# The final norm of an encoder layer, taken by halves of a row, with the reciprocal root applied on ScalarE and VectorE

## The chip, the cores and the metric

The kernel runs on one core of one Trainium2 chip. Its metric is the device time of one execution in microseconds (us). A core has TensorE (PE, with its weight loads as PEld), VectorE (DVE), ScalarE (ACT), GpSimd (POOL) and SyncE (SP), each with an instruction stream of its own that runs in order; they wait for one another through semaphores. Work arrays lie in SBUF, in 128 partitions; products of TensorE arrive in PSUM, here 8 banks of 128x512 f32.

## What is computed

One layer of a bidirectional encoder on 768 tokens (a group of 512 and one of 256) of width 1024: a token mixer, a feed-forward block, and a last RMSNorm. Cut to what matters here:

```
def rmsnorm(x, w):
    xf = x.astype(F32)
    y = xf * lax.rsqrt(jnp.mean(xf * xf, axis=-1, keepdims=True) + EPS)
    return (y * w.astype(F32)).astype(x.dtype)

    for l in range(DEPTH):                      # DEPTH is 1
        h = h + token_mixer(rmsnorm(h, norm_mix[l]), ...)
        h = h + conv_ffn(rmsnorm(h, norm_ffn[l]), ...)
    return rmsnorm(h, norm_final)
```

The mean of the squares runs over a whole row of 1024, so no element of a row can leave before the row's last residual is added. The weight `norm_final` does not depend on the mean.

## The kernel before, in words

The tokens are six tiles of 128 (`NT` = 6), the width is 8 pieces of 128. `h[:, t, :]` is the residual row of tile `t`, 128x1024 f32, in SBUF from the middle of the program on. Each matrix product is made of three passes of float32r halves (hi, lo), so a weight comes from HBM into `raw`, is split by ScalarE (`split_hi`, `hi_unit`) and VectorE (`split_lo`, `lo_unit`) into `ring`, and TensorE reads it there.

The feed-forward block works in three chunks of `FF`, with 8, 8 and 6 blocks of 128. After each chunk, `down` multiplies the gated activations `g` by the down weights and VectorE adds the result to `h` (`residual`, L1122). It does so in two halves of the output columns: first columns 0 to 511 for all six tiles, then columns 512 to 1023. In the last chunk the second half runs tile by tile (`by_token`): TensorE makes 18 matmuls of 128x512 for tile 0 and counts `down_done` up, then 18 for tile 1, and so on. The order in every stream is written out by hand; no scheduler moves anything.

Behind the last chunk stands the final norm. `wfin`, the weights of it in all partitions, is loaded over `af` as soon as the last product that reads `af` is done. Then, tile by tile, in this order:

- VectorE adds the second half of the row (L1122);
- ScalarE squares the row of 1024 into `junk2` and sums it into `stat[:, 0, t]` (L786);
- VectorE divides by 1024 and adds EPS (`variance`, L800), ScalarE takes the root (L788), VectorE the reciprocal (L1317);
- VectorE multiplies the row of 1024 by the reciprocal and by `wfin`, in place in `h` (L1319), and counts `out_ready` up;
- SP, which waits for that, issues the store of the tile to `y_s` or `y_p` (L396). The program ends when all six stores have landed.

Of the kernel before, what the change touches and what calls it, by code (L numbers as in the profile page):

```python
# [30 lines left out]
ALU = mybir.AluOpType  # L31
ACT = mybir.ActivationFunctionType
F32 = mybir.dt.float32
# [3 lines left out]
P = 128  # L37
D = 1024
KD = D // P
NS, NP = 512, 256  # L40
T = NS + NP
NT = T // P
# [6 lines left out]
EPS = 1e-6  # L49
STRIP = NS + 3 * P  # L50
UNIT = 1024
HALF = T // 2
HK = KD // 2
PIECE = UNIT // 2
CHUNKS = ((0, 8), (8, 16), (16, 22))
# [29 lines left out]
ORD, PLACE, UPLACE, FREED, PIECES = {}, {}, {}, {}, {}  # L85
# [79 lines left out]
def build(nc, x_s, x_p, units, pairs, vec, w_final, ident_d, masks_d, rot_d, strips_d, y_s, y_p):  # L165
    with ExitStack() as ctx:
        def sem(name):
            return ctx.enter_context(nc.semaphore(name))

        def persistent(name, shape, dtype=F32):  # L170
            return ctx.enter_context(nc.sbuf_tensor(name, shape, dtype))

        def region(*tensors):

            with ExitStack() as phase:
                return [phase.enter_context(nc.sbuf_tensor(n, s, d)) for n, s, d in tensors]
# [2 lines left out]
        ring = persistent("ring", [P, 8, 2, PIECE], F32R)  # L179
        ident = persistent("ident", [P, P])  # L180
        vecs = persistent("vecs", [P, V_N])
        stat = persistent("stat", [P, 4, NT])

        hn, x_in, xn, y32, junk = region(
            ("hn", [P, 2, KD, T], F32R),
# [13 lines left out]
        _, osq, _, kT = region(  # L199
            ("d0", [P, 2 * KD * T + KD * T + 2048 + 2 * T + 7 * P + T], F32), ("osq", [P, 2, T], F32),  # L200
            ("d1", [P, 10 * T], F32), ("kT", [P, T], F32))
# [5 lines left out]
        _, merged = region(("n2", [P, 2 * KD * T], F32), ("merged", [P, 2, KD, T], F32R))  # L207


        h, hxn, hy = region(("h", [P, NT, D], F32), ("hxn", [P, 2, D], F32), ("hy", [P, 6, KD, P], F32))  # L210
        _, g, raw2, tb, u2, v2, cb, mid, af = region(
            ("b0", [P, NT, D], F32), ("g", [P, 2, 8, T], F32R), ("raw2", [P, 2, UNIT], F32), ("tb", [P, 2, PIECE], F32),
            ("u2", [P, 2, T], F32), ("v2", [P, T], F32), ("cb", [P, T], F32), ("mid", [P, HALF], F32),
            ("af", [P, 7, 2, HK, HALF], F32R))
        *_, wfin, junk2 = region(
            ("c0", [P, NT * D + 2 * 8 * T + 3072 + 4 * T + HALF], F32), ("wfin", [P, D], F32), ("junk2", [P, D], F32))

        _, sums0 = region(
            ("e0", [P, NT * D + 2 * 8 * T + 3072 + 4 * T + HALF], F32), ("sums0", [P, 7, 2, HK, HALF], F32))
# [6 lines left out]
        vec_ld, mix_ld, strip_ld, fin_ld, out_st = sem("vec_loaded"), sem("mix_loaded"), sem("strip_loaded"), sem("fin_loaded"), sem("out_stored")  # L226
# [3 lines left out]
        sq_done, var_done, sd_done, xn_done, tr_done, y_done, yhi_done, ylo_done = (  # L230
            sem(n) for n in ("sq_done", "var_done", "sd_done", "xn_done", "tr_done", "y_done", "yhi_done", "ylo_done"))
# [11 lines left out]
        w_done, h_up = sem("wout_done"), sem("h_updated")  # L243
# [5 lines left out]
        s_done, s_last, fyhi, fylo = sem("tokens_combined"), sem("last_tokens_combined"), sem("forms_hi"), sem("forms_lo")  # L249
        p1_cp, p12_cp, p13_cp = sem("first_copied"), sem("second_copied"), sem("third_copied")  # L250
        c11_dn, c22_dn, c12_dn = sem("c11_done"), sem("c22_done"), sem("c12_done")
        dn, out_rdy = sem("down_done"), sem("out_ready")

        raws = (raw, raw2)

# [66 lines left out]
        @blk.sync  # L322
        def _(sp):
            def load(n, parity):

                after(sp, lo_split, n - 1)
                src = units[n] if isinstance(n, int) else units[at(n), :, :].rearrange("a p n -> (a p) n")
                sp.dma_start(raw[:, parity, :], src).then_inc(raw_ld[parity], 16)

            xs = x_s.rearrange("(t p) d -> t p d", p=P)  # L330
            xp = x_p.rearrange("(t p) d -> t p d", p=P)
            for t in range(NT):
                sp.dma_start(x_in[:, t, :], xs[t] if t < 4 else xp[t - 4]).then_inc(x_ld[t], 16)

            def mixer_loads(hd):
                for u in range(U_MIX):
                    load(hd * U_MIX + u, u % 2)
                    if u == 5:

                        after(sp, rp, 12 * hd)  # L340
                        src = strips_d[hd] if isinstance(hd, int) else strips_d[at(hd), :, :].rearrange("a p n -> (a p) n")
                        sp.dma_start(strips[:].rearrange("p a n -> p (a n)"), src).then_inc(strip_ld, 16)

            mixer_loads(0)
            with sp.Fori(1, HEADS_H) as hd:
                mixer_loads(hd)
            with sp.Fori(U_HG // 2, (U_O0 + 4) // 2) as i:
                load(2 * i, 0)
                load(2 * i + 1, 1)

            sp.wait_ge(unit_done, U_O0)
            sp.dma_start(h[:, 0:4, :], x_s.rearrange("(t p) d -> p t d", p=P)).then_inc(h_ld, 16)
            sp.dma_start(h[:, 4:6, :], x_p.rearrange("(t p) d -> p t d", p=P)).then_inc(h_ld, 16)

            with sp.Fori((U_O0 + 4) // 2, U_D // 2) as i:
                load(2 * i, 0)
                load(2 * i + 1, 1)

            def load_pair(i, prior, plain):

                b = raw_of(i)
                if prior is not None:
                    sp.wait_ge(flo, ORD[prior, A22] + 1)
                else:
                    sp.wait_ge(lo_split, plain + 1)
                sp.dma_start(raws[b][:, 0, :], pairs[i, 0]).then_inc(pu_ld[b], 16)
                if prior is not None:
                    sp.wait_ge(flo, ORD[prior, S4] + 1)
                sp.dma_start(raws[b][:, 1, :], pairs[i, 1]).then_inc(pv_ld[b], 16)

            for lo, hi in CHUNKS:
                for i in range(lo, hi):
                    if i == 1:

                        sp.wait_ge(w_done, 2 * NT)
                        sp.dma_start(raw2[:, 0, :], pairs[i, 0]).then_inc(pu_ld[1], 16)
                        sp.dma_start(raw2[:, 1, :], pairs[i, 1]).then_inc(pv_ld[1], 16)
                    elif i == 0 or i == lo + 1:
                        load_pair(i, None, U_D + lo - 1)
                    else:  # L380
                        load_pair(i, i - 2, None)
                last_raw = hi - 1 if raw_of(hi - 1) == 0 else hi - 2
                for n in range(U_D + lo, U_D + hi):
                    if n < U_D + lo + 2:
                        sp.wait_ge(flo, ORD[last_raw, S4] + 1)
                    else:
                        sp.wait_ge(lo_split, n - 1)
                    sp.dma_start(raw[:, n % 2, :], units[n]).then_inc(raw_ld[n % 2], 16)

            sp.wait_ge(fdone, len(ORD))  # L390
            sp.dma_start(wfin[:], w_final).then_inc(fin_ld, 16)
            ys = y_s.rearrange("(t p) d -> t p d", p=P)
            yp = y_p.rearrange("(t p) d -> t p d", p=P)
            for t in range(NT):
                sp.wait_ge(out_rdy, t + 1)
                sp.dma_start(ys[t] if t < 4 else yp[t - 4], h[:, t, :]).then_inc(out_st, 16)  # L396
            sp.wait_ge(out_st, 16 * NT)


# [1 line left out]
        def _(act):  # L401
# [353 lines left out]
            for lo, hi in CHUNKS:  # L755
# [25 lines left out]
                for n in range(U_D + lo, U_D + hi):  # L781
                    hi_upto(UPLACE[n] + 6)
            for t in range(NT):
                act.wait_ge(h_up, (2 + 2 * len(CHUNKS)) * NT - NT + t + 1)
                act.drain()
                act.activation(junk2[:], h[:, t, :], ACT.Square, accum_out=stat[:, 0, t:t + 1]).then_inc(sq_done, 1)  # L786
                act.wait_ge(var_done, 2 * NT + t + 1)
                act.activation(stat[:, 2, t:t + 1], stat[:, 1, t:t + 1], ACT.Sqrt).then_inc(sd_done, 1)  # L788


        @blk.vector
        def _(dve):
# [5 lines left out]
            def variance(t, base):  # L798
                dve.wait_ge(sq_done, base + t + 1)
                dve.tensor_scalar(stat[:, 1, t:t + 1], stat[:, 0, t:t + 1], 1.0 / D, EPS, ALU.mult,  # L800
                                  ALU.add).then_inc(var_done, 1)
# [472 lines left out]
            for c, (lo, hi) in enumerate(CHUNKS):  # L1274
# [32 lines left out]
                if c + 1 < len(CHUNKS):  # L1307
                    for t in range(NT):
                        dve.wait_ge(dn, 2 * NT * c + NT + t + 1)
                        residual(t, 1, t)  # L1310
            dve.wait_ge(fin_ld, 16)
            for t in range(NT):
                dve.wait_ge(dn, (2 * len(CHUNKS) - 1) * NT + t + 1)
                residual(t, 1, t)
                variance(t, 2 * NT)
                dve.wait_ge(sd_done, 2 * NT + t + 1)
                dve.reciprocal(stat[:, 3, t:t + 1], stat[:, 2, t:t + 1])  # L1317
                dve.drain()
                dve.scalar_tensor_tensor(out=h[:, t, :], in0=h[:, t, :], scalar=stat[:, 3, t:t + 1], in1=wfin[:],  # L1319
                                         op0=ALU.mult, op1=ALU.mult).then_inc(out_rdy, 1)  # L1320


        @blk.gpsimd
# [501 lines left out]
```

## Time and profile before

| | us |
|---|---|
| median of 3 runs | 1285.16 |
| the runs | 1284.92 to 1285.38 |
| the profiled execution, its own time | 1284.88 |
| its span, first to last instruction | 1283.1 |
| mean granted TensorE clock | 0.996 |

The profiled execution took 1.8 us more than its span, which lies outside the instructions, and 0.28 us less than the median. TensorE is busy for nearly the whole span; busy times of the others overlap it. The profile page divides the span into 40 slices of 32 us, so the whole final norm lies in the last slice, and it has to be read from the timeline. In a row of the timeline or of the chain the first number is the start and the second the length, both in us from the span's start; in brackets stands how long the engine had been idle, and what ended that.

### The profile page before, as it was taken

Reading aid. Unit: us, or ns where it says so; the run is one execution under the profiler, and the core shown is the slowest. Engines: PE = TensorE matmul, PEld = TensorE weight load, DVE = VectorE, ACT = ScalarE, POOL = GpSimd, SP = SyncE. Lnnn points to the kernel's source line nnn. Section 1 sums busy time; section 2 is a strip of 40 time slices with the busy share of each in tenths; the row PEclk is TensorE's granted clock in tenths of the full one; section 3 lists DMA queues with packets and bytes.
Section 4 is the critical chain, followed back from the end, with each engine's and each line's share of the span. In section 5 each row is a group of like instructions: output and inputs, shape, how many; then the busy total and the mean of one; then the engine's idle time right before and its main releaser. Section 6 shows DMA issues by size and latency. Waiting matters only on the chain.

```text
span 1283.1 us, 17974 instructions
## 1 busy us (share of the span) xinstructions
PE 1251.8 (98%) x7088; PEld 1127.2 (88%) x7088; DVE 708.1 (55%) x956; ACT 484.4 (38%) x706; POOL 129.0 (10%) x93
## 2 busy tenths in 40 slices
PE   6999999999999999999999989999999999999997
PEld 5999999899999988888888879998789998799976
DVE  7494585486377372232223697765237764347654
ACT  5352253335144152122211355553125553135522
POOL 0000000000000000000000304420133420223200
PEclk9999999999999999999999998999999999999999
DMA  4311211101211112212124122122202213112122
GB/s 168 134 42 42 74 38 50 61 33 49 78 33 49 34 50 66 66 50 68 63 67 164 33 66 66 66 66 82 82 34 66 77 55 125 40 37 79 50 82 98
DMA packets 23179, 86.09 MB, mean 67 GB/s; under 512 B 2512, under 2 KB 2768, under 8 KB 23120
## 3 DMA queue, kind: packets, MB, share of 16 engines
q1 hardware_dynamic: 22544, 83.90, 19.0%
q10 hardware_dynamic: 576, 1.38, 0.3%
q8 instruction: 41, 0.67, 0.2%
q14 instruction: 18, 0.15, 0.0%
HBM read 82.12 MB, written 3.15 MB: 66 GB/s over the span
## 4 chain that ended last, share of the span: by engine, by line
PE 94%; DVE 4%; ACT 1%; DVEq 1%; issue 1%; DMA 0%; SPq 0%; ACTq 0%
PE ps L1397 58%; PE ps L1641 24%; PE ps L1494 3%; PE ps L1434 3%; PE ps L1487 1%; PE ps L1504 1%; PE ps L1422 1%; DVE af L1182 1%; PE ps L1424 1%; DVE h L1122 1%; DVE ring L1135 1%; PE ps L1379 0%; PE ps L1470 0%; PE ps L1475 0%; PE ps L1479 0%
## 5 line engine op out<-in xcount | busy, mean ns | idle before, releaser
L1397 PE MATMUL ps<-hn,ring 128*128 128x256 f32 (+1 forms) x2544 | 466.8, 338 | 0.3 <-DVE hn L824 0.3
L1397 PEld LDWEIGHTS ps<-hn,ring 128*128 128x128 f32 x2544 | 387.2, 189 | 51.6 <-issue 0.7
L1641 PE MATMUL ps<-af,ring 128*128 128x384 f32 x1848 | 332.6, 341 | 10.8 <-DVE v L1219 5.6
L1641 PEld LDWEIGHTS ps<-af,ring 128*128 128x128 f32 x1848 | 328.3, 189 | 14.9 <-issue 5.9
L1397 PE MATMUL ps<-ring,g 128*128 128x512 f32 x792 | 186.7, 397 | 0.8 <-issue 0.8
L1397 PEld LDWEIGHTS ps<-ring,g 128*128 128x128 f32 x792 | 148.9, 188 | 37.8 <-issue 2.0
L795 DVE TENSOR_TENSOR ring<-raw,ring 128x1024 fp32r<-128x1024 f32 x68 | 83.1, 1224 | 122.1 <-ACT ring L409 117.7
L458 ACT ACTIVATE sig<-ps 128x768 f32<-128x768 f32 x36 | 29.2, 810 | 183.1 <-PE ps L1397 183.0
L409 ACT ACTIVATE ring<-raw 128x1024 fp32r<-128x1024 f32 x68 | 71.6, 1055 | 29.8 <-PE ps L1397 10.6
L1135 DVE TENSOR_TENSOR ring<-raw,ring 128x512 fp32r<-128x512 f32 x88 | 73.4, 869 | 16.7 <-ACT ring L646 16.6
L1356 POOL TENSOR_TENSOR sums<-raw 128x512 f32<-128x512 f32 x1 | 1.3, 1295 | 713.8 <-DMA raw<-in_pairs 713.8
L1397 PE MATMUL ps<-gated,ring 128*128 128x512 f32 (+1 forms) x384 | 69.1, 338 | 0.0
L1397 PE MATMUL ps<-ring,merged 128*128 128x512 f32 x288 | 68.8, 398 | 0.1
L1397 PEld LDWEIGHTS ps<-gated,ring 128*128 128x128 f32 x384 | 59.6, 188 | 8.8
L1397 PEld LDWEIGHTS ps<-ring,merged 128*128 128x128 f32 x288 | 53.8, 188 | 13.2 <-issue 0.5
L873 DVE TENSOR_TENSOR pt<-ps,strips 128x512 f32<-128x512 f32 (+1 forms) x48 | 28.5, 601 | 66.1 <-PE ps L1424 66.1
L646 ACT ACTIVATE ring<-raw 128x512 fp32r<-128x512 f32 x88 | 52.3, 622 | 30.2 <-PE ps L1397 30.2
L1122 DVE TENSOR_TENSOR h<-ps,h 128x512 f32<-128x512 f32 x48 | 33.1, 690 | 42.7 <-PE ps L1397 42.2
L471 ACT ACTIVATE yc<-tree_k 128x768 f32<-128x768 f32 x28 | 25.6, 916 | 76.6 <-DVE tree_k L960 41.2
L1135 DVE TENSOR_TENSOR ring<-tb,ring 128x512 fp32r<-128x512 f32 x63 | 43.4, 693 | 17.8 <-ACT ring L646 17.8
L1227 DVE SCALAR_TENSOR_TENSOR cb<-u,vecs,cb 128x511 f32<-128x511 f32 x88 | 50.2, 612 | 2.0 <-issue 0.4
L1140 DVE TENSOR_TENSOR ring<-raw,ring 128x1024 fp32r<-128x1024 f32 x22 | 27.6, 1264 | 40.9 <-ACT ring L653 40.9
(151 smaller groups left out, 1210.1 us busy)
## 6 DMA issues: line engine op xcount, KB each, us to landing
raw<-in_units SPq DMA_DIRECT2D x90, 512.0 KB, 3.5
raw<-in_pairs SPq DMA_DIRECT2D x44, 512.0 KB, 3.4
strips<-in_strips SPq DMA_DIRECT2D x4, 896.0 KB, 4.5
x_in<-in_x_s SPq DMA_DIRECT2D x4, 512.0 KB, 5.4
h<-in_x_s SPq DMA_DIRECT2D x1, 2048.0 KB, 8.3
y_s<-h SPq DMA_DIRECT2D x4, 512.0 KB, 2.6
x_in<-in_x_p SPq DMA_DIRECT2D x2, 512.0 KB, 7.5
h<-in_x_p SPq DMA_DIRECT2D x1, 1024.0 KB, 10.4
```

The costliest lines, as they stand in the source:

```text
L409: act.activation(ring[:, 2 * slot:2 * slot + 2, 0, :], pieces(raw[:, slot % 2, :]), ACT.Copy).then_inc(hi_split, 1)
L458: ins = act.activation(sig[:, u % 2, :], dense(u), ACT.Sigmoid)
L646: act.activation(place_of(i, x, 0), source(i, x), ACT.Copy).then_inc(fhi, 1)
L795: dve.tensor_tensor(ring[:, 2 * slot:2 * slot + 2, 1, :], pieces(raw[:, slot % 2, :]), ring[:, 2 * slot:2 * slot + 2, 0, :].bitcast(F32), ...
L873: dve.tensor_tensor(pt[:, (i % 4) * NS:(i % 4) * NS + width], ps[:, 4 + i % 2, 0:width], strips[:, a, c0:c0 + width], ALU.mult).then_inc(r ...
L1122: return dve.tensor_tensor(hs, ps[:, bank, :], hs, ALU.add).then_inc(h_up, 1)
L1135: dve.tensor_tensor(place_of(i, x, 1), source(i, x), place_of(i, x, 0).bitcast(F32), ALU.subtract).then_inc(flo, 1)
L1227: ins = dve.scalar_tensor_tensor(out=cs, in0=u2[:, i % 2, c0 + frm:c0 + frm + w - 1], scalar=vecs[:, V_CONV + tap * NF + i:V_CONV + tap * ...
L1397: ins = pe.matmul(out, w if stationary_w else x, x if stationary_w else w, start=start and i == 0, stop=stop and i == 2)
L1434: ins = pe.matmul(ps[:, 6 + m // 4, col:col + 64], pt[:, (i % 4) * NS + c * P:(i % 4) * NS + (c + 1) * P], rv[:, m * P + 64 * a:m * P + 64 ...
L1494: ins = pe.matmul(out(c * P, P), yc[:, c * P:(c + 1) * P], facing(tree_q[:], what, c * P, P), start=True, stop=True)
L1641: ins = pe.matmul(ps[:, bank, 0:HALF], ring[:, p, a, k * P:(k + 1) * P], af[:, x, b, k, :], start=first and k == 0 and j == 0, stop=k == H ...
```

## The change

`stat` gets two more rows (4 and 5), `junk2` is halved, and a new tile `hw` (six rows of 1024) takes the weighted row; it lies over `af`, as `wfin` does. Four semaphores are new, and `out_first_half_ready`.

Ahead of the last six residuals, when the first halves of all rows are final, ScalarE squares the six first halves (into `stat[:, 4]`), VectorE multiplies the six first halves by `wfin` into `hw`, and then makes of the six sums a scaled sum plus EPS in one 128x6 instruction (`stat[:, 5]`). Per tile there is then: the residual, a multiplication of the second half by `wfin` into `hw` on VectorE, the square of the second half on ScalarE beside it, the variance (with `stat[:, 5, t]` where EPS stood), root and reciprocal as before. The reciprocal is applied by both engines: ScalarE scales the first half of `hw`, VectorE the second, each in place, and SP waits for both.

```
-        stat = persistent("stat", [P, 4, NT])
+        stat = persistent("stat", [P, 6, NT])
...
-            ("c0", [P, NT * D + 2 * 8 * T + 3072 + 4 * T + HALF], F32), ("wfin", [P, D], F32), ("junk2", [P, D], F32))
+            ("c0", [P, NT * D + 2 * 8 * T + 3072 + 4 * T + HALF], F32), ("wfin", [P, D], F32), ("junk2", [P, PIECE], F32), ("hw", [P, NT, D], F32))
...
             for t in range(NT):
+                sp.wait_ge(out_rdy0, t + 1)
                 sp.wait_ge(out_rdy, t + 1)
-                sp.dma_start(ys[t] if t < 4 else yp[t - 4], h[:, t, :]).then_inc(out_st, 16)
+                sp.dma_start(ys[t] if t < 4 else yp[t - 4], hw[:, t, :]).then_inc(out_st, 16)
...
             for t in range(NT):
+                act.wait_ge(h_up, (1 + 2 * len(CHUNKS)) * NT - NT + t + 1)
+                act.wait_ge(fdone, len(ORD))
+                act.drain()
+                act.activation(junk2[:], h[:, t, 0:PIECE], ACT.Square, accum_out=stat[:, 4, t:t + 1]).then_inc(half_sq, 1)
+            for t in range(NT):
                 act.wait_ge(h_up, (2 + 2 * len(CHUNKS)) * NT - NT + t + 1)
                 act.drain()
-                act.activation(junk2[:], h[:, t, :], ACT.Square, accum_out=stat[:, 0, t:t + 1]).then_inc(sq_done, 1)
+                act.activation(junk2[:], h[:, t, PIECE:D], ACT.Square, accum_out=stat[:, 0, t:t + 1]).then_inc(sq_done, 1)
                 act.wait_ge(var_done, 2 * NT + t + 1)
                 act.activation(stat[:, 2, t:t + 1], stat[:, 1, t:t + 1], ACT.Sqrt).then_inc(sd_done, 1)
+                act.wait_ge(root_done, t + 1)
+                act.wait_ge(weighed, t + 1)
+                act.activation(hw[:, t, 0:PIECE], hw[:, t, 0:PIECE], ACT.Copy, scale=stat[:, 3, t:t + 1]).then_inc(out_rdy0, 1)
...
             dve.wait_ge(fin_ld, 16)
+            dve.wait_ge(fdone, len(ORD))
+            dve.drain()
+            for t in range(NT):
+                dve.tensor_tensor(hw[:, t, 0:PIECE], h[:, t, 0:PIECE], wfin[:, 0:PIECE], ALU.mult).then_inc(weighed, 1)
+            dve.wait_ge(half_sq, NT)
+            dve.tensor_scalar(stat[:, 5, :], stat[:, 4, :], 1.0 / D, EPS, ALU.mult, ALU.add).then_inc(half_var, 1)
             for t in range(NT):
                 dve.wait_ge(dn, (2 * len(CHUNKS) - 1) * NT + t + 1)
                 residual(t, 1, t)
-                variance(t, 2 * NT)
+                dve.drain()
+                dve.tensor_tensor(hw[:, t, PIECE:D], h[:, t, PIECE:D], wfin[:, PIECE:D], ALU.mult).then_inc(weighed, 1)
+                dve.wait_ge(sq_done, 2 * NT + t + 1)
+                dve.wait_ge(half_var, 1)
+                dve.tensor_scalar(stat[:, 1, t:t + 1], stat[:, 0, t:t + 1], 1.0 / D, stat[:, 5, t:t + 1], ALU.mult,
+                                  ALU.add).then_inc(var_done, 1)
                 dve.wait_ge(sd_done, 2 * NT + t + 1)
-                dve.reciprocal(stat[:, 3, t:t + 1], stat[:, 2, t:t + 1])
-                dve.drain()
-                dve.scalar_tensor_tensor(out=h[:, t, :], in0=h[:, t, :], scalar=stat[:, 3, t:t + 1], in1=wfin[:],
-                                         op0=ALU.mult, op1=ALU.mult).then_inc(out_rdy, 1)
+                dve.reciprocal(stat[:, 3, t:t + 1], stat[:, 2, t:t + 1]).then_inc(root_done, 1)
+                dve.wait_ge(root_done, t + 1)
+                dve.tensor_scalar(hw[:, t, PIECE:D], hw[:, t, PIECE:D], stat[:, 3, t:t + 1], None, ALU.mult).then_inc(out_rdy, 1)
```

On VectorE, from the six residuals of the first halves to the store of tile 0, the stream read so before (`h_updated` counts residuals, `down_done` the tiles that TensorE has finished):

```order
L1122 TENSOR_TENSOR h<-ps,h 128x512 [waits down_done] x6
L1122 TENSOR_TENSOR h<-ps,h 128x512 [waits down_done,fin_loaded]
L800 TENSOR_SCALAR stat<-stat 128x1 [waits sq_done]
L1317 RECIPROCAL stat<-stat 128x1 [waits sd_done]
L1319 SCALAR_TENSOR_TENSOR h<-h,stat,wfin 128x1024
```

In the changed kernel the same stretch of VectorE reads:

```order
L1132 TENSOR_TENSOR h<-ps,h 128x512 [waits down_done] x6
L1325 TENSOR_TENSOR hw<-h,wfin 128x512 [waits product_done,fin_loaded]
L1325 TENSOR_TENSOR hw<-h,wfin 128x512 x5
L1327 TENSOR_SCALAR stat<-stat 128x6 [waits half_squares]
L1132 TENSOR_TENSOR h<-ps,h 128x512 [waits down_done]
L1332 TENSOR_TENSOR hw<-h,wfin 128x512
L1335 TENSOR_SCALAR stat<-stat 128x1 [waits half_variance,sq_done]
L1338 RECIPROCAL stat<-stat 128x1 [waits sd_done]
L1340 TENSOR_SCALAR hw<-hw,stat 128x512 [waits root_inverted]
```

Seven instructions stand newly between the last first-half residual and the first second-half one, and a tile has five instructions on VectorE where it had four.

On ScalarE a tile of the final norm read so before (the table load stands there once, in tile 0):

```order
L786 ACTIVATE junk,stat<-h 128x1024 [waits h_updated]
L788 ACT_TABLE_LOAD
L788 ACTIVATE stat<-stat 128x1 [waits var_done]
```

And now, with the six early squares ahead of it:

```order
L789 ACTIVATE junk,stat<-h 128x512 [waits product_done,h_updated] x6
L793 ACTIVATE junk,stat<-h 128x512 [waits h_updated]
L795 ACT_TABLE_LOAD
L795 ACTIVATE stat<-stat 128x1 [waits var_done]
L798 ACTIVATE hw<-hw,stat 128x512 [waits out_weighed,root_inverted]
```

A tile's square is half as long, and a scaling copy stands behind its root. TensorE's, GpSimd's and SP's streams have the same instructions in the same order, but for the source and the second wait of the stores. All tiles that are placed behind `stat` in SBUF (every one but `raw`, `ring`, `ident`, `vecs` and `stat`) start 64 bytes later in each partition.

## Rows read from the trace of the kernel before

**Rows 1.** The page, busy time of each engine and its share of the span.

```profile
PE 1251.8 (98%) x7088; PEld 1127.2 (88%) x7088; DVE 708.1 (55%) x956; ACT 484.4 (38%) x706; POOL 129.0 (10%) x93
```

**Rows 2.** The chain that ended last, from 1230 us: start, length, what.

```profile
1250.58 25.54 PE ps L1397 x108
...
1276.14 0.70 DVE h L1122
...
1276.92 1.16 ACT junk L786 x2
...
1278.10 0.16 DVE stat L800
...
1278.29 0.21 ACT stat L788
...
1278.52 0.16 DVE stat L1317
1278.68 0.03 DVEq L1318
```

**Rows 3.** The timeline from 1276 us: the last tile's last steps and stores.

```profile
1275.86 4.54 SPq L396 DMA_DIRECT2D y_p<-h  x2
...
1276.92 1.06 ACT L786 ACTIVATE junk<-h 128x1024 f32<-128x1024 f32 x1 [2.64 <-DVE h L1122]
1277.88 0.19 ACT L786 ACTIVATION_READ_ACCUMULATOR junk<-h 128x1 f32 x1
...
1278.76 1.28 DVE L1319 SCALAR_TENSOR_TENSOR h<-h,stat,wfin 128x1024 f32<-128x1024 f32 x1
```

**Rows 4.** DMA issues of the stretch 1276.1 to 1283.1: count, KB each, us to landing.

```profile
y_p<-h SPq DMA_DIRECT2D x2, 512.0 KB, 2.6
```

**Rows 5.** The issues of the last two stores: durations ns, first and last start.

```profile
L396 SPq DMA_DIRECT2D y_p<-h x2: 332/332/332, 1275.9 to 1280.1; - x2
```

**Rows 6.** Groups of instructions, shapes apart: count, busy us, mean ns of one.

```profile
L409 ACT ACTIVATE ring<-raw 128x1024 fp32r<-128x1024 f32 x68 | 71.6, 1055 | 29.8 <-PE ps L1397 10.6 <-PEq L1605 7.4 <-DMA raw<-in_units 6.7
L646 ACT ACTIVATE ring<-tb 128x512 fp32r<-128x512 f32 x63 | 37.0, 620 | 33.4 <-PEq L1735 14.6 <-PE ps L1397 14.6 <-DVE tb L1157 3.7
L720 ACT ACTIVATE cb<-u,vecs 128x384 f32<-128x384 f32 x22 | 15.5, 705 | 0.0
L496 ACT ACTIVATE rv<-ps 128x768 f32<-128x768 f32 x4 | 3.2, 812 | 10.9 <-PE ps L1479 10.9
L504 ACT ACTIVATE oT<-ps,vecs 128x768 f32 x3 | 2.7, 902 | 5.8 <-PE ps L1475 5.8
L307 DVE TENSOR_TENSOR hy<-hy 128x512 f32<-128x512 f32 x2 | 1.4, 693 | 0.2
L810 DVE TENSOR_SCALAR xn<-x_in,stat 128x1024 f32<-128x1024 f32 x6 | 4.5, 754 | 0.5
L816 DVE TENSOR_TENSOR y<-ps,vecs 128x1024 f32<-128x1024 f32 x6 | 7.3, 1220 | 1.3 <-PE ps L1379 1.3
L901 DVE TENSOR_SCALAR hstat<-hstat 128x6 f32<-128x6 f32 x4 | 0.7, 172 | 0.3
```

**Rows 7.** The timeline from 1225 us: residuals, first tile's norm, tile 4's residual.

```profile
1246.85 4.20 DVE L1122 TENSOR_TENSOR h<-ps,h 128x512 f32<-128x512 f32 x6 [2.52 <-PE ps L1397]
...
1255.13 0.69 DVE L1122 TENSOR_TENSOR h<-ps,h 128x512 f32<-128x512 f32 x1 [4.08 <-PE ps L1397]
1255.90 1.06 ACT L786 ACTIVATE junk<-h 128x1024 f32<-128x1024 f32 x1 [12.83 <-DVE h L1122]
...
1257.07 1.28 ACT L788 ACT_TABLE_LOAD   x1
...
1271.93 0.69 DVE L1122 TENSOR_TENSOR h<-ps,h 128x512 f32<-128x512 f32 x1 [0.32 <-PE ps L1397]
```

**Rows 8.** Busy time by stretch: PE, PEld, DVE, ACT, POOL, clock, DMA share, GB/s.

```profile
1250.50:1255.10 4.60, 4.52 (x20) 3.69 (x21) 0.55 (x1) 0.00 (x0) 0.00 (x0) 1.00 0.00 0
1255.10:1276.10 21.00, 21.00 (x90) 16.57 (x88) 11.23 (x20) 8.06 (x16) 0.00 (x0) 1.00 0.25 100
```

**Rows 9.** The load of the final weights: its issue in the timeline.

```profile
1234.39 0.43 SPq L391 DMA_DIRECT2D wfin<-in_w_final  x1
```

**Rows 10.** The load of the final weights: time to landing, by the tile's view.

```profile
DMA to landing us min/median/max: 6.5/6.5/6.5
```

More of the change, by code:

```diff
@@ L214, in build @@
             ("af", [P, 7, 2, HK, HALF], F32R))
-        *_, wfin, junk2 = region(
-            ("c0", [P, NT * D + 2 * 8 * T + 3072 + 4 * T + HALF], F32), ("wfin", [P, D], F32), ("junk2", [P, D], F32))
+        *_, wfin, junk2, hw = region(
+            ("c0", [P, NT * D + 2 * 8 * T + 3072 + 4 * T + HALF], F32), ("wfin", [P, D], F32), ("junk2", [P, PIECE], F32), ("hw", [P, NT, D], F32))
         _, sums0 = region(
@@ L251, in build @@
         c11_dn, c22_dn, c12_dn = sem("c11_done"), sem("c22_done"), sem("c12_done")
-        dn, out_rdy = sem("down_done"), sem("out_ready")
+        dn, out_rdy, out_rdy0 = sem("down_done"), sem("out_ready"), sem("out_first_half_ready")
+        half_sq, half_var, root_done, weighed = sem("half_squares"), sem("half_variance"), sem("root_inverted"), sem("out_weighed")
         raws = (raw, raw2)
```

## The prediction, made before the changed kernel ran

> **What bounds the kernel now.** I read the page first: TensorE is busy for 98% of the span, VectorE for 55%, ScalarE for 38% [rows 1]. An edit on VectorE and ScalarE can therefore pay only where TensorE is not running. TensorE's stream and its waits are untouched. The chain that ended last shows where it stops: a run of 108 matmuls ends at 1276.12 us, and behind it stand, one after the other, the last tile's residual, square, variance, root, reciprocal and the final multiplication [rows 2, 3]. The final multiplication ends at 1280.04 us (1278.76 + 1.28), the last store is issued at 1280.07 (the two issues end at 1280.40, each takes 0.33), and it lands 2.6 us later [rows 3 to 5]. So the span of 1283.1 us splits into 1276.1 in which TensorE sets the pace, 3.9 us of a serial chain for one tile, and 3.0 us of store and end. The change can shorten only those 3.9 us, unless it moves TensorE's end. That caps the whole effect near 0.3% of the time, and the true effect is below that, since half of the chain's links stay.
>
> **The path of the last tile, step by step.** I count from the residual's start at 1276.14 us [rows 2], because VectorE is idle there before and will be after.
>
> 1. Residual: 0.69 us, unchanged. ScalarE starts its square at 1276.92.
> 2. Square: now 512 elements instead of 1024. Before, the variance started 1.18 us behind the square's start (1276.92 to 1278.10) [rows 2]. The square took 1.06 us there, the same as ScalarE's plain copy of 1024 elements (1055 ns), and a copy of 512 takes 620 ns [rows 6, 3]. So half a row saves 0.435 us, and the accumulator read (0.19) stays. The variance can start at 1277.67.
> 3. Multiplication of the second half by the weights, new on VectorE, ahead of the variance. It waits for the residual and a drain; the same drain took 0.08 us behind the reciprocal (1278.68 to 1278.76) [rows 2, 3]. So it starts at 1276.91 and, at 0.69 us as for two SBUF operands of 128x512 [rows 6], ends at 1277.60. It lies under the square with 0.07 us to spare. That is the thinnest cover in the sum: if this step starts or runs 0.1 us later, only some hundredths appear on the path.
> 4. Variance, root, reciprocal: 0.58 us from 1278.10 to 1278.68 [rows 2], the same three instructions; the variance reads its addend from SBUF instead of an immediate, for which I take nothing and allow 0.05. The reciprocal ends at 1278.25.
> 5. Applying the reciprocal. Before: 1.28 us on VectorE for 1024 elements with two multiplications. Now there are two legs side by side. ScalarE: a copy of 512 with a scale read per partition. No row shows that form. The low end is the unscaled copy, 620 ns. The high end comes from the scaled and biased one of 384 elements, 705 ns, plus 128 elements at 0.85 ns (the slope from 620 to 1055 ns): 813 ns. Between them, the copy of 768 with such a scale takes 902 ns against 812 without, 0.09 us more [rows 6]. This is the same operation, so I take 0.62 + 0.09 = 0.71. With 0.04 us from VectorE's end to ScalarE's start (as between variance and root, 1278.25 to 1278.29), ScalarE ends at 1279.00. VectorE: a wait of 0.08 and a 128x512 multiplication by a scalar. Low end: half of the 754 ns that 1024 elements take; high end: 0.69, as two tensors; I take 0.754 less half of the 0.53 that two tensors of 1024 cost over 512 (1220 less 693 ns), since the 754 ns show about two elements in the time of one: 0.49 us [rows 6]. VectorE ends at 1278.82, before ScalarE, which sets the end.
> 6. SP waits for two semaphores; the later one is ScalarE's, and the other has been counted by then. I take no more than the 0.03 us that it took before. The store is issued at about 1279.04.
>
> The store now leaves 1.03 us earlier (1280.07 to 1279.04). For small handshakes that the rows don't show I take off 0.03, so **the gain is 1.0 us**. Bounds of the sum: ScalarE's leg at 0.62 gives 1.1; at 0.81, with 0.1 for a late weight multiplication and variance and 0.1 for extra waits, it gives 0.7.
>
> On step 5 the row shows a price for the scale, 90 ns in 812 [rows 6]. The Trainium skill, page "ScalarE: Activation LUTs", section "Step-by-step: what each stage is for", calls scale and bias a "free affine" that is applied ahead of the lookup, in each instruction; by that the leg would take 0.62 us and the time would be 1284.1. The trace speaks against it here, so the sum keeps the 0.09.
>
> **What lies ahead of the last tile, and its cover.** The six early squares start behind the first residuals (1246.85 on), where ScalarE is idle for 12.8 us [rows 7]. Each takes about 0.62 + 0.19 and a gap, 0.87 us, so all are done by about 1252.9. The six multiplications follow the six residuals that end at 1251.05, six times 0.69 and gaps, to about 1255.3; the weights landed at 1240.9 [rows 7, 9, 10]. The 128x6 instruction (0.17 us, as another of that shape [rows 6]) brings it to 1255.6. Before, the residual of tile 0 started at 1255.13 [rows 7], so tile 0 is now late by 0.4 to 0.5 us: the cover of 4.08 us of idle VectorE is used up and a little more. What absorbs the lag is TensorE's rhythm: 108 matmuls in 25.54 us are six tiles of 4.25 us, and the new chain of a tile holds VectorE for 2.7 us (1276.14 to 1278.82), where the old one held it for 3.9. Even with the table load of 1.28 us in tile 0 [rows 7], VectorE is free near 1259.4, when tile 1 arrives. From there on it waits for TensorE on every tile, as before only in the last two (0.32 and 0.31 us idle) [rows 7]. Nothing of the lag is left at 1276.14. TensorE doesn't wait for any of this: its tiles write banks whose last readers are the first-half residuals, done by 1251.05. I also price contention at nothing, because TensorE held its pace with VectorE busy for 11.2 and ScalarE for 8.1 of 21 us, at a granted clock of 1.00 in both stretches [rows 8].
>
> **The sum.** The profiled execution would be 1284.88 - 1.0 = 1283.9 us, its span 1282.1. It stood 0.28 below the median, so the median goes from 1285.16 to **1284.2 us**, 0.08% less.
>
> **Rivals.**
> - *The instruction count tells.* A tile has one more instruction on each engine and three more waits. If fixed parts of them come onto the path, 0.15 us each on two engines (a 693 ns operation of 512 elements against 1220 of 1024 leaves about 0.16 us that doesn't scale [rows 6]), the gain is 0.7 and the time 1284.5. For it speaks the 0.07 us of cover in step 3; against it, that path and kernel have the same number of links, and the additions lie beside them. The Trainium skill's page "VectorE: DVE Perf Modes", section "The TRN2 errata — SBUF-src ops pay a fixed extra latency per instruction", speaks against halves in this way: many small operations pay the fixed part each time. The rows agree with a fixed part; they don't put it on this path.
> - *It doesn't do what it says.* The two legs don't overlap but run one after the other (ScalarE's scaling behind VectorE's), say because a wait falls on the wrong one. Then step 5 takes 0.08 + 0.49 + 0.04 + 0.71 = 1.32 against 1.36, and only the square's 0.43 remains: 1284.7. The order of waits speaks against it, since both legs wait for the reciprocal alone.
> - *Slower: the moved tiles.* Everything behind `stat` starts 64 bytes later, also `hn`, `g` and `af`, which TensorE reads in nearly all of its 7088 matmuls. Should such a read cost more at the new start, it is on the path all the time. The point from which it decides is 1.0 us / 7088 = 0.14 ns for each matmul; at 0.5 ns the time would be 1285.16 - 1.0 + 3.5 = 1287.7. It can as well go the other way. Nothing in the trace varies with a start address, so I give it little.
> - *A new end on VectorE.* If its scalar multiplication ran like a two-tensor one and its waits cost 0.2 more, its leg ends at 1279.2 instead of ScalarE's 1279.0: 1284.4, inside the forecast's bounds.
>
> **How the numbers follow.** The forecast with the last rival, 1284.0 to 1284.5: 74%. The instruction count: 10%, 1284.5 to 1284.8. Legs in series or another lost overlap: 5%, up to 1285.2. Moved tiles: 8%, of which half beyond 0.2% slower and 1 in 100 faster by more than that. 3% for what I haven't seen. The runs before lie within 0.23 us of their median, which is as wide as the forecast's own bounds; with that and a small effect of the moved tiles either way, the range is 1283.4 to 1285.3. A measurement of this kernel can tell about 0.2% (2.6 us) from no change. The mechanism can't reach that: chances 0.02 faster, 0.94 same, 0.04 slower.
>
> **What would show it.** In the changed profile: TensorE's last matmul within 0.3 us of 1276.1 from the start; then square about 0.62 us, variance 1.53 us behind the residual's start (1.96 before), the reciprocal's end 2.11 behind it (2.54 before), ScalarE's scaled copy last at 2.86, the store at 2.9 (3.93 before). Tile 0's residual 0.4 to 0.5 us later than before, and VectorE idle ahead of each later one. The forecast is wrong if the variance waits for the weight multiplication instead of the square, if the scaled copy takes over 0.9 us, or if TensorE's end moves by more than the 1.0 us in question.

## The result, and the profile after

| | before | changed kernel |
|---|---|---|
| median, us | 1284.79 (6 runs) | 1277.76 (6 runs) |
| the runs, us | 1283.63 to 1285.38 | 1275.41 to 1278.74 |
| profiled execution, us | 1284.88 | 1277.07 |
| its span, us | 1283.1 | 1275.3 |

The ratio of the times is 0.9943, with a 95% interval of 0.9933 to 0.9954. The forecast was 1284.2 in a range of 1283.4 to 1285.3; the kernel is 7.0 us faster, not 1.0.

The page of the changed kernel, busy time of each engine, answers to [rows 1]:

```profile
PE 1244.8 (98%) x7088; PEld 1120.5 (88%) x7088; DVE 711.9 (56%) x969; ACT 490.8 (38%) x724; POOL 129.1 (10%) x93
```

VectorE and ScalarE have become busier by 4 and 6 us, as they should with more instructions. TensorE has the same 7088 matmuls and is busy for 7 us less. The timeline of the changed kernel from 1269 us (start, length, what, idle time before it) shows the last tile, to be laid beside [rows 2, 3]:

```profile
1269.31 0.69 DVE L1132 TENSOR_TENSOR h<-ps,h 128x512 f32<-128x512 f32 x1 [1.28 <-PE ps L1417]
1270.08 0.63 ACT L793 ACTIVATE junk<-h 128x512 f32<-128x512 f32 x1 [1.82 <-DVE h L1132]
1270.09 0.69 DVE L1332 TENSOR_TENSOR hw<-h,wfin 128x512 f32<-128x512 f32 x1
1270.62 0.19 ACT L793 ACTIVATION_READ_ACCUMULATOR junk<-h 128x1 f32 x1
1270.84 0.21 DVE L1335 TENSOR_SCALAR stat<-stat 128x1 f32<-128x1 f32 x1
1271.09 0.20 ACT L795 ACTIVATE stat<-stat 128x1 f32<-128x1 f32 x1 [0.28 <-DVE stat L1335]
1271.32 0.16 DVE L1338 RECIPROCAL stat<-stat 128x1 f32<-128x1 f32 x1 [0.27 <-ACT stat L795]
1271.52 0.72 ACT L798 ACTIVATE hw<-hw,stat 128x512 f32<-128x512 f32 x1 [0.23 <-DVE stat L1338]
1271.52 0.49 DVE L1340 TENSOR_SCALAR hw<-hw,stat 128x512 f32<-128x512 f32 x1
1272.27 0.33 SPq L398 DMA_DIRECT2D y_p<-hw  x1
```

From the residual's start to the store's issue it is 2.96 us, where it was 3.93. That is the 0.97 us that the change was to bring. But the residual itself starts at 1269.31 instead of 1276.14: 6.8 us of the gain lie before the norm, in TensorE's stream, which the diff doesn't touch. The chain that ended last tells where. First before (start, length, what; L1641 is the product that streams `af` through weights from `ring`, L1397 here the down product, which streams `ring` through weights from `g`):

```profile
772.71 100.44 PE ps L1641 x552
...
946.44 114.98 PE ps L1641 x648
...
1066.49 33.73 PE ps L1397 x144
...
1134.75 85.20 PE ps L1641 x480
```

and of the changed kernel (L1661 and L1417 are the same two lines):

```profile
770.77 98.10 PE ps L1661 x552
...
941.83 114.86 PE ps L1661 x648
...
1061.68 33.60 PE ps L1417 x144
...
1129.65 83.72 PE ps L1661 x480
```

The same 480 matmuls in a row, with nothing between them, take 83.72 us instead of 85.20: 174.4 ns each instead of 177.5. The difference is spread over the program. By the starts in the two chains, TensorE gains 1.94 us up to the row of 552, 2.41 in the `af` products of the first chunk from there on, 0.20 in the second chunk's, 1.57 in the third's, and 0.26, 0.29 and 0.16 in the three down products; the sum is 6.83. No wait of any size has gone; the matmuls themselves follow one another faster: 1817 neighbouring `af` matmuls are 177.4 ns apart before and 1821 are 175.3 ns apart after. The granted clock isn't it: 0.996 before and 0.997 after.

### The profile page after: what moved, and what is told of

Read it like the earlier page. It is cut to its first block, busy times and chain, and to the rows that moved or that the text cites. A ratio compares the mean times of both kernels' runs of the same rounds, so it can differ in the third digit from the quotient of the medians.

```text
span 1275.3 us, 18036 instructions
## 1 busy us (share of the span) xinstructions
PE 1244.8 (98%) x7088; PEld 1120.5 (88%) x7088; DVE 711.9 (56%) x969; ACT 490.8 (38%) x724; POOL 129.1 (10%) x93
## 4 chain that ended last, share of the span: by engine, by line
PE 94%; DVE 4%; ACT 1%; DVEq 1%; issue 1%; DMA 0%; SPq 0%; ACTq 0%
PE ps L1417 58%; PE ps L1661 24%; PE ps L1514 3%; PE ps L1454 3%; PE ps L1507 1%; PE ps L1524 1%; PE ps L1442 1%; DVE af L1192 1%; PE ps L1444 1%; DVE h L1132 1%; DVE ring L1145 1%; PE ps L1399 0%; PE ps L1490 0%; PE ps L1499 0%; PE ps L1495 0%
## 5 line engine op out<-in xcount | busy, mean ns | idle before, releaser
L1417 PE MATMUL ps<-hn,ring 128*128 128x256 f32 (+1 forms) x2544 | 465.2, 338 | 0.3 <-DVE hn L834 0.3
L1417 PEld LDWEIGHTS ps<-hn,ring 128*128 128x128 f32 x2544 | 385.7, 189 | 51.6 <-issue 0.7
L1661 PE MATMUL ps<-af,ring 128*128 128x384 f32 x1848 | 328.2, 340 | 11.1 <-DVE v L1229 5.6
L1661 PEld LDWEIGHTS ps<-af,ring 128*128 128x128 f32 x1848 | 324.0, 189 | 15.1 <-issue 5.9
L1417 PE MATMUL ps<-ring,g 128*128 128x512 f32 x792 | 186.0, 395 | 0.8 <-issue 0.8
L1417 PEld LDWEIGHTS ps<-ring,g 128*128 128x128 f32 x792 | 148.4, 188 | 37.6 <-issue 2.0
L805 DVE TENSOR_TENSOR ring<-raw,ring 128x1024 fp32r<-128x1024 f32 x68 | 83.2, 1224 | 121.4 <-ACT ring L411 117.0
L1417 PE MATMUL ps<-gated,ring 128*128 128x512 f32 (+1 forms) x384 | 68.8, 338 | 0.0
L1417 PE MATMUL ps<-ring,merged 128*128 128x512 f32 x288 | 68.6, 397 | 0.1
L1417 PEld LDWEIGHTS ps<-gated,ring 128*128 128x128 f32 x384 | 59.3, 188 | 8.8
L1417 PEld LDWEIGHTS ps<-ring,merged 128*128 128x128 f32 x288 | 53.6, 188 | 13.1 <-issue 0.5
```

Source lines behind the costliest of these rows:

```text
L805: dve.tensor_tensor(ring[:, 2 * slot:2 * slot + 2, 1, :], pieces(raw[:, slot % 2, :]), ring[:, 2 * slot:2 * slot + 2, 0, :].bitcast(F32), ...
L1417: ins = pe.matmul(out, w if stationary_w else x, x if stationary_w else w, start=start and i == 0, stop=stop and i == 2)
L1661: ins = pe.matmul(ps[:, bank, 0:HALF], ring[:, p, a, k * P:(k + 1) * P], af[:, x, b, k, :], start=first and k == 0 and j == 0, stop=k == H ...
```

## Experiments

In what follows "pace" is the mean time from one matmul's start to the next one's in the trace, over all neighbours of one kind less than 300 ns apart. It is worked out from the starts and doesn't depend on modelled ends.

**Is it the norm's code or the tiles' place?** One of the rivals was that every tile behind `stat` starts 64 bytes later. Two kernels split the change into its two parts. The first is the kernel before with the shift alone:

```
-        stat = persistent("stat", [P, 4, NT])
+        stat = persistent("stat", [P, 6, NT])
```

> The kernel before with nothing changed but stat at six rows (two unused), so that every tile behind it starts 64 bytes later, as in the changed kernel. Theory A (the start address of the tiles that TensorE reads sets its pace): this alone gives the larger part, 1278.5 to 1279.5 us, its last matmul near 1269.5 and the tail still 7.0 us long. Theory B (the new instructions of the norm or their places in the program did it): 1284.8, no gain. Theory C (the executions vary by themselves): anything between, and the runs of one kernel would spread over both.

The second is the changed kernel with its two new rows of sums in a small tile, `early`, behind `hw`, and `stat` as it was:

```
-        stat = persistent("stat", [P, 6, NT])
+        stat = persistent("stat", [P, 4, NT])
...
-        *_, wfin, junk2, hw = region(
+        *_, wfin, junk2, hw, early = region(
...
-            dve.tensor_scalar(stat[:, 5, :], stat[:, 4, :], 1.0 / D, EPS, ALU.mult, ALU.add).then_inc(half_var, 1)
+            dve.tensor_scalar(early[:, 1, :], early[:, 0, :], 1.0 / D, EPS, ALU.mult, ALU.add).then_inc(half_var, 1)
```

> The changed kernel with its two new rows of sums in a small tile of their own behind hw, so that stat keeps four rows and every tile starts where it did before. Theory A: only the shorter tail is left, 1283.8 us (1.0 below the kernel before), with TensorE's last matmul at 1276.1 from the start. Theory B: the whole gain, 1277.8.

Measured: the shift alone 1278.61 us (ratio 0.9948, 0.9931 to 0.9964). The norm alone 1284.21 us against 1284.86 of the kernel before (0.9995, 0.9985 to 1.0004), so its gain can't be told from nothing by the times. The trace of it tells: TensorE's end has not come forward (the last residual starts at 1276.54, 0.4 us later than in the kernel before), and the store is issued 2.96 us behind it.

```profile
1276.54 0.69 DVE L1132 TENSOR_TENSOR h<-ps,h 128x512 f32<-128x512 f32 x1 [1.29 <-PE ps L1417]
...
1278.75 0.72 ACT L798 ACTIVATE hw<-hw,stat 128x512 f32<-128x512 f32 x1 [0.23 <-DVE stat L1338]
1278.75 0.49 DVE L1340 TENSOR_SCALAR hw<-hw,stat 128x512 f32<-128x512 f32 x1
1279.50 0.33 SPq L398 DMA_DIRECT2D y_p<-hw  x1
```

Theory A holds: the place of the tiles gave 6.2 of the 7 us. Theory B, by which the norm's new instructions gave the whole gain, falls: they shorten the tail by about what they were priced at and leave TensorE's pace as it was. The runs of each kernel keep to themselves, 1277.04 to 1279.17 us and 1283.40 to 1284.71, which speaks against theory C.

**Other shifts, the norm left as it was before.** Only the number of rows of `stat` changes: 5 rows place the tiles 32 bytes later, 9 rows 128, 14 rows 256.

> The kernel before with all tiles behind stat 32 bytes later, which makes their starts whole multiples of 64 bytes; they were 32 off that before, and are 32 off it with a shift of 64. Theory A in the form that an address relative to 64 bytes counts: another time than either, 1277 to 1290, and the shift of 64 would then not have changed anything. In the form that the place in a longer period (128 or 256 bytes) counts: 1279 to 1285. Theory B: 1284.8.

> The kernel before with all tiles behind stat 128 bytes later. Theory A: 1284.8 if the place within 128 bytes decides, 1278 to 1285 if a longer period does. Theory B: 1284.8. Theory C: within the spread of the others.

> The kernel before with all tiles behind stat 256 bytes later. Period of 256 bytes (or a shorter one that divides it): 1284.8, the 648 af products in 115.0 us. A longer period, or none: another time, most likely 1276 to 1281.

Measured: 1280.68 us (ratio 0.9969), 1276.36 (0.9936) and 1284.49 (0.9997, 0.9987 to 1.0006). The expectation that a place within 64 or within 128 bytes decides has fallen, since 64 and 128 are both unlike 0 and unlike each other. A shift of 256 gives the old kernel's pace again:

```profile
1134.02 76.58 PE ps L1641 x432
...
1250.16 25.55 PE ps L1397 x108
```

The 432 take 177.3 ns each, and the last 108 take 25.55 us as in [rows 2]. Among the shifts tried the period is 256 bytes.

**The place itself, or the place against another tile?** Everything moves by 128 bytes, `raw` and `ring` too:

```
+        persistent("ahead", [P, 32])
         raw = persistent("raw", [P, 2, UNIT])
```

> The kernel before with everything 128 bytes later, raw and ring too, so that no tile moves against another. Theory A1 (what counts is how the tile that TensorE streams lies against the tile it loads its weights from, of which one is always ring): 1284.8 us, the 648 af products in 115.0 us. Theory A2 (the absolute start of the tile counts): 1276.4, as for a shift of 128 bytes behind stat, and the 648 in 112.8.

Measured: 1284.81 us (ratio 1.0, 0.9991 to 1.001), TensorE's pace as before. The chain has again:

```profile
1066.11 33.73 PE ps L1398 x144
...
1134.33 85.23 PE ps L1642 x480
```

The same shift that saves 8.5 us when `ring` stays saves nothing when `ring` goes with it. So the start of a tile is nothing in itself; the distance between the two tiles that TensorE reads in one matmul is what counts (A1). In the dense products one of the two is always `ring`: as weights in the mixer and in the `af` products, as streamed operand in `w_out` and the down products.

**One tile at a time.** Only `af` moves, by 128 bytes, by a gap of 32 floats ahead of it:

> The kernel before with only af (and the tiles laid over it) 128 bytes later; hn, merged, g and ring stay. Theory A: the products that stream af get the whole of their gain, about 3.3 ns for each of 1752 matmuls or 5.8 us, and the down products (g) and the mixer (hn, merged) nothing: 1279.0 us. If another tile than the one TensorE reads were behind it, no gain: 1284.8.

Only `g` moves, by 160 bytes; what lies behind it moves by 256, which is no move:

> The kernel before with g alone 160 bytes later, on the ring's place within 256 bytes; what lies behind it 256 bytes later, which was the kernel before's place again. g is where the down products load their weights, and ring is what they stream, the other way round than with af. Theory A1, each pair by itself: the 792 down matmuls go from 234.2 to 227.0 ns (5.7 us) and nothing else changes: 1279.1 us. If the place of the streamed tile alone counted: 1284.8.

Measured: 1279.12 us (0.9954, 0.9938 to 0.9971) and 1279.26 us (0.9957, 0.9940 to 0.9973), each within 0.2 us of its expectation. In the first the third chunk's 468 `af` matmuls take 173.9 ns each, and the down product is what it was:

```profile
1062.33 33.73 PE ps L1397 x144
...
1130.55 81.37 PE ps L1641 x468
```

In the second it is the other way round: 226.8 ns instead of 234.2 for each down matmul, `af` untouched:

```profile
1065.03 32.66 PE ps L1397 x144
...
1131.13 85.17 PE ps L1641 x480
```

**The whole period.** The changed kernel with 9, 8, 10, 12 and 13 rows in `stat`, shifts of 128, 96, 160, 192 and 224 bytes against the kernel before:

> The changed kernel with nine rows in stat, so that its tiles start 128 bytes later than in the kernel before (64 later than in the changed kernel). If the shift and the shorter tail add: 1276.4 - 0.9 = 1275.4 us, which beats both kernels. If the two don't add: 1277 or more.

> The changed kernel with eight rows in stat: tiles behind it 96 bytes later than in the kernel before. Theory A1 (the place of the streamed tile against the weights' tile within 256 bytes sets TensorE's pace) says only that the time belongs to this place; between the places 64 (af products 173.6 to 177.0 ns each) and 128 (173.8) I expect 173.6 to 174 for af and 1275 to 1277 us. If places that are whole multiples of 64 bytes from the ring's (0, 32 behind before) run another way: af 176.4, g 232.4, and 1279.8, as at a shift of 32.

> The same with ten rows: 160 bytes later, which is the tiles' start on a multiple of 256 bytes from the ring's. Theory A1 with two streams that get in each other's way when they start on the same place: the slowest, 1284 us or more. If equal places are the good ones: 1275 or less. The two would tell what the good distance is.

> The same with twelve rows: 192 bytes later, 32 past the ring's place. Between the neighbours: 1275 to 1284 us; with no guess inside that, since nothing run so far lies there.

> The same with thirteen rows: 224 bytes later, 32 bytes short of the whole period, which is the kernel before's place again. A place's effect from both neighbours: 1280 to 1284 us; a multiple of 64 from the ring's place (as with 32) would give 1279.8.

The table has all eight places. The distance is the start of the streamed tile less that of the weights' tile, modulo 256. It follows from the sizes in the kernel: `ring`, `ident`, `vecs` and the large tiles are whole multiples of 256 bytes and `stat` takes 96, so the tiles behind it start 96 bytes plus the shift past `ring`'s place. The row of 32 comes from the kernel with the old norm. Where both norms ran at one place (64 and 128), their paces agree to 0.2 ns. The kernels ran at four different times, each beside the kernel before, whose median was between 1284.70 and 1284.86 us each time.

| shift | median, us | distance, `hn` and `af` streamed | `hn`, ns | `af`, ns | distance, `ring` streamed | `g`, ns |
|---|---|---|---|---|---|---|
| 0 (halves_no_shift) | 1284.21 | 96 | 172.1 | 177.4 | 160 | 234.2 |
| 32 (old norm) | 1280.68 | 128 | 171.8 | 176.7 | 128 | 232.4 |
| 64 (changed kernel) | 1277.76 | 160 | 171.3 | 175.3 | 96 | 233.3 |
| 96 | 1268.73 | 192 | 169.7 | 175.2 | 64 | 228.9 |
| 128 | 1274.99 | 224 | 171.5 | 174.2 | 32 | 233.3 |
| 160 | 1265.47 | 0 | 170.2 | 174.1 | 0 | 227.0 |
| 192 | 1276.30 | 32 | 170.6 | 175.1 | 224 | 233.3 |
| 224 | 1269.94 | 64 | 169.4 | 174.1 | 192 | 233.3 |

The ratios of the five new ones are 0.9924 (shift 128), 0.9878 (96), 0.9853 (160), 0.9938 (192) and 0.9881 (224), each within 0.0018 either way. For 128 the sum of shift and norm came out (1275.4 expected, 1274.99 measured). Two guesses were clearly wrong: the shifts of 96 and 224 were far better than between their neighbours. The one for 192 held (1275 to 1284 expected), but was too wide to tell anything, and of the two opposite guesses for 160 the second held. Equal places are best for `g`, and as good as any for `af`.

The column of `hn` mixes matmuls of 512 and of 256 columns, and they don't agree on a place. Taken over neighbours of one width, those of 512 take 228.9 ns at a distance of 0, 229.7 at 64 and 232.6 to 233.8 at the other six, much as `g` does. Those of 256 take 117.0 ns at 192 and 121.7 at 0, where the wider ones are best. So the number of columns decides which distance is good, together with the distance itself. At the shift of 160 the last two halves of the down product and the last chunk's `af` products read:

```profile
1119.42 81.36 PE ps L1661 x468
...
1208.17 24.52 PE ps L1417 x108
...
1232.96 24.78 PE ps L1417 x108
```

The last 108 take 24.78 us against 25.54 in [rows 2].

**Each tile on its best place.** The table's rows differ in which tile they suit: `hn`, both widths taken together, is best at a distance of 64, `g` at 0. Starting from the shift of 160, a gap of 16 floats goes ahead of `hn` (and with it of all that is placed relative to it, `gated` among them), and `merged` gets 64 floats instead, to stay at a distance of 0 and clear of `hn`:

```
-            ("hn", [P, 2, KD, T], F32R),
+            ("gap1", [P, 16], F32), ("hn", [P, 2, KD, T], F32R),
...
-        _, merged = region(("n2", [P, 2 * KD * T], F32), ("merged", [P, 2, KD, T], F32R))
+        _, merged = region(("n2", [P, 2 * KD * T + 64], F32), ("merged", [P, 2, KD, T], F32R))
```

> The changed kernel with every tile on the place that ran best so far for it: hn and gated (streamed) 64 bytes past the ring's place, as in the shift of 224; merged, g and af on the ring's place, as in the shift of 160. Each pair by itself: hn from 170.2 to 169.4 ns a matmul (2426 of them, 1.9 us), the rest as with 160: 1263.5 us. If the pairs are not independent: 1265.5 or more.

Measured: 1262.74 us (1262.39 to 1262.99; ratio 0.9830, 0.9814 to 0.9847), 22 us under the kernel before and 15 under the changed kernel. The pace of `hn` went from 170.2 to 169.2 ns, those of `af` (174.0) and `g` (227.0) stayed. Unrounded, the difference is 1.08 ns; for 2544 matmuls that is 2.7 us, the whole difference to the shift of 160 (1265.47 us). As far as this shows the pairs are independent, and this version beats both kernels.

## Why the prediction was wrong

**What was right: the sum of the tail.** Predicted gain 1.0, measured 0.97. Step by step, from the residual's start: variance at 1.53 (forecast 1.53), reciprocal's end at 2.17 (2.11), ScalarE's scaled copy done at 2.93 (2.86), store at 2.96 (2.90). The missing 0.06 is the variance itself: 0.21 us with its addend from SBUF, where I had taken the 0.15 of the immediate and allowed 0.05. The scaled copy took 0.72 (0.71 forecast between 0.62 and 0.81), VectorE's scaling 0.49 (0.49). The row on the scale's price was the right one to follow. The price that the prediction derived from "free affine" was a misreading: the same page of the Trainium skill, "ScalarE: Activation LUTs", states in its section "What ACT_TABLE_LOAD costs" that each [128,1] pointer operand adds about 93 ns. The trace agrees: 0.72 us against 0.62 for the unscaled copy [rows 6]. The weight multiplication ended at 1270.78, 0.06 us ahead of the variance, so its thin cover held on the last tile. The rivals of the instruction count, of legs in series and of a new end on VectorE fell: both scalings start in the same moment, 1271.52, and VectorE's ends first.

That the cover held is in part luck. One tile earlier it didn't:

```profile
1265.10 0.69 DVE L1132 TENSOR_TENSOR h<-ps,h 128x512 f32<-128x512 f32 x1 [1.50 <-PE ps L1417]
1266.26 0.69 DVE L1332 TENSOR_TENSOR hw<-h,wfin 128x512 f32<-128x512 f32 x1 [0.46 <-issue]
1266.86 0.21 DVE L1335 TENSOR_SCALAR stat<-stat 128x1 f32<-128x1 f32 x1
```

Here the multiplication starts 1.16 us behind the residual instead of 0.78, and the variance 1.76 behind it instead of 1.53. The other seven kernels with the new norm show the same delay at this tile, and at no other. What causes it isn't shown; on the last tile it would have taken 0.23 us of the 0.97, by these rows.

**A small miss: tile 0.** I had the residual of tile 0 late by 0.4 to 0.5 us. It is not late: it starts 4.47 us behind the first of the last 108 matmuls (1243.83 to 1248.30), where it was 4.55 before (1250.58 to 1255.13, [rows 2, 7]). The timeline of the changed kernel:

```profile
1243.83 25.44 PE L1417 MATMUL ps<-ring,g 128*128 128x512 f32 x108 [0.26 <-issue]
...
1244.39 3.70 DVE L1325 TENSOR_TENSOR hw<-h,wfin 128x512 f32<-128x512 f32 x6
...
1248.01 0.17 DVE L1327 TENSOR_SCALAR stat<-stat 128x6 f32<-128x6 f32 x1
1248.30 0.69 DVE L1132 TENSOR_TENSOR h<-ps,h 128x512 f32<-128x512 f32 x1
```

I took 0.69 us and gaps for each of the six multiplications. Between SBUF operands with no wait they overlap: 3.70 us for six, 0.62 each. The cover was enough, which changed nothing in the sum.

**The step that failed: TensorE's end taken as fixed, and the rival "moved tiles" left out of the sum.** The sum keeps the last residual at 1276.14, because TensorE's stream is untouched; it started at 1269.31, 6.8 us earlier, which the prediction itself had named as a sign of being wrong. The rival named the mechanism's place rightly (64 bytes, `hn`, `g` and `af`, all 7088 matmuls) and its leverage too (0.14 ns for each matmul is worth 1 us). It failed in its sign and its weight. I took it as a danger of being slower, at 8%, and gave 1 in 100 to its being faster beyond 0.2%. The measured effect is 0.96 ns a matmul, 6.8 us, a gain. The reason I gave, that nothing in the trace varies with a start address, was no evidence: in one kernel each pair of tiles has one distance, so the trace could not have shown it. Between kernels it does vary: the 512-column matmul of the down product, at 234.2 ns in the kernel before, takes 227.0 at the shift of 160. Nor was another engine behind the 234.2, as two windows of the kernel before show, both at a granted clock of 1.00 (columns as in [rows 8]):

```profile
1251.20:1255.00 3.80, 3.80 (x18) 3.07 (x17) 0.00 (x0) 0.00 (x0) 0.00 (x0) 1.00 0.00 0
1256.00:1275.00 19.00, 19.00 (x82) 15.26 (x81) 9.71 (x19) 7.96 (x16) 0.00 (x0) 1.00 0.28 110
```

The first has neither VectorE nor ScalarE nor a DMA in it, the second has all of them; the pace in them is 233.7 and 234.2 ns. The kernel with `g` alone moved has such a quiet stretch too:

```profile
1246.70:1250.40 3.70, 3.70 (x18) 3.05 (x17) 0.00 (x0) 0.00 (x0) 0.00 (x0) 1.00 0.00 0
```

Its pace is 228.6 ns. So the gain is there while no other engine works, and it comes and goes with the distance between the two tiles that TensorE reads. What is left is that TensorE gets in its own way, between the stream that it multiplies and the weights that it loads at the same time; the two reads themselves are in no trace. A range that took this rival seriously, both ways, would have been several us wide on each side of 1284.2.

**What stays open.** Why a distance is good or bad isn't shown, nor why the number of columns changes which one is: the worst for streamed `af` at 384 columns is 96, while `hn` at 512 has its worst at 160 (233.8 ns) as streamed `ring` has (234.2). For `g`, 64 and 192 are far apart (228.9 and 233.3). At some places the pace also isn't one number. At the changed kernel's, the second chunk's 648 `af` products took 114.86 us, as slow as before, while those of the first and third chunk were faster, in both profiled kernels with this place (174.5, 177.0 and 173.9 ns by chunk, against 177.7, 177.1 and 177.4 before). At the shift of 192 it is the first chunk that is slow: 177.0, 173.8 and 174.2. The runs of the changed kernel spread over 3.3 us, those with 192 over 3.2 and those with 96 over 3.2, where the shifts of 128 and 160 stayed within 1.1. That the spread is chunks which fall to the one pace or the other fits, but wasn't tried.

## What to carry to other kernels

Where TensorE sets the time, look at where the streamed tile and the weights' tile start, modulo 256 bytes, before tuning anything by a microsecond, and try the eight places in steps of 32 bytes: here they span 19 us, 1.5%. Matmuls of different widths can want different places, so look at each pair of tiles. Any edit that changes the size of a small tile allocated ahead of the large ones moves them all; compare two kernels with the placement held, or the gain will be put down to the wrong part. The edit of the tail, a chain of 3.9 us, was summed from rows to within 0.1 us here.

## What the runs showed of the hardware

- TensorE's pace depends on the distance between its two SBUF reads, with a period of 256 bytes among the shifts tried: 227.0 to 234.2 ns for 512 columns of float32r, 174.1 to 177.4 for 384, 117.0 to 121.7 for 256. The Trainium skill's page "SBUF — State Buffer", section "Who interferes with whom", gives TensorE two independent read ports, one for the moving operand and one for the weight load, and states that it never waits for anyone. The runs agree on the other engines (the two windows of the kernel before) and not on the two ports: the measurement decides, and the pace isn't independent of how the two reads lie.
- Moving both tiles together by 128 bytes changes nothing (1284.81 against 1284.77 us), where moving only the tiles behind `stat` by as much saves 8.5. This is the one such move tried.
- A ScalarE copy of 512 with a scale read per partition takes 0.72 us, 0.10 over the plain one; a 128x1 instruction of VectorE 0.21 us with its addend read from SBUF, 0.15 with an immediate; a VectorE multiplication of 512 by such a scalar 0.49 us; six two-operand multiplications of 512 in a row 0.62 us each, though one alone shows 0.69.
